# A fused decoder step on one core: value products of the attention one step later in TensorE's order, and a head's gate behind the decode maximum on VectorE

## The reference

```
def _attend_block(q_lat, q_pe, c_kv, k_pe, q_pos, k_pos):
    s = (einsum('bqhc,bkc->bhqk', q_lat, c_kv)
         + einsum('bqhr,bkr->bhqk', q_pe, k_pe)) * ATTN_SCALE
    s = where(k_pos <= q_pos, s, -inf)
    p = softmax(s, axis=-1)
    return einsum('bhqk,bkc->bqhc', p, c_kv)
...
    o = einsum('bthc,chv->bthv', o_lat, w_uv)
    return (o * silu(gate)) @ w_out
```

## Time and profile before

| | |
|---|---|
| median of 3 runs | 1121.33 us |
| lowest, highest | 1116.54, 1121.57 us |
| profiled execution, its own time | 1121.29 us |
| its span, first to last instruction | 1119.1 us |
| mean granted TensorE clock | 0.967 |
| TensorE busy | 1041.1 us (93%) |
| VectorE busy | 514.5 us (46%) |
| ScalarE busy | 308.0 us (28%) |
| GpSimd busy | 93.8 us (8%) |

### The profile page before, as it was taken

How to read it: one execution, slowest core, us unless ns; L and a number is a source line. 1 busy time by engine, 2 the same in 40 slices (tenths; PEclk the granted TensorE clock), 3 DMA queues, 4 the chain that set the end, 5 groups by cost and what they waited for, 6 DMA issues and landing times.

```text
span 1119.1 us, 26006 instructions
## 1 busy us (share of the span) xinstructions
PE 1041.1 (93%) x11635; PEld 740.6 (66%) x11635; DVE 514.5 (46%) x963; ACT 308.0 (28%) x589; POOL 93.8 (8%) x140
## 2 busy tenths in 40 slices
PE   2697999999999999999999798999899999999996
PEld 0476877767677777767655344888584767666566
DVE  0595445464555546455555786220202354444105
ACT  2213132232322132232210214232223344444102
POOL 0002011010100111010010130000001000100111
PEclk8899999999999999999989898999999899999989
DMA  8601012040402203040050657311324222432102
GB/s 355 232 1 61 17 63 95 2 155 3 150 8 79 79 11 146 2 155 3 11 226 19 246 212 290 152 56 57 109 74 97 76 95 96 146 139 89 63 1 77
DMA packets 19999, 110.49 MB, mean 99 GB/s; under 512 B 7080, under 2 KB 11952, under 8 KB 13872
## 3 DMA queue, kind: packets, MB, share of 16 engines
q1 hardware_dynamic: 13712, 84.62, 20.4%
q0 software_dynamic: 2304, 20.97, 5.2%
q10 hardware_dynamic: 3872, 3.24, 0.9%
HBM read 102.30 MB, written 5.19 MB: 96 GB/s over the span
## 4 chain that ended last, share of the span: by engine, by line
PE 80%; DVE 7%; ACT 2%; issue 2%; DMA 1%; SPq 0%; ACTq 0%; DVEq 0%
PE pj L959 20%; PE pj L1437 7%; PE bk L1069 7%; PE pj L1348 5%; PE pj L1488 3%; PE pj L1201 3%; PE pj L1366 2%; PE bk L1540 2%; PE bk L1468 2%; PE bk L892 2%; PE bk L1524 2%; PE bk L1525 2%; PE bk L1142 1%; PE pj L1553 1%; PE pj L988 1%
## 5 line engine op out<-in xcount | busy, mean ns | idle before, releaser
L959 PE MATMUL pj<-XM,ring 128*128 128x260 f32 x1024 | 261.7, 397 | 0.9 <-DVE XM L1784 0.9
L959 PEld LDWEIGHTS pj<-XM,ring 128*128 128x128 f32 x1024 | 183.7, 190 | 40.7 <-issue 12.1
L1437 PE MATMUL pj<-XM,ring 128*128 128x260 f32 x352 | 79.3, 388 | 2.9 <-ACT XM L777 2.9
L1437 PEld LDWEIGHTS pj<-XM,ring 128*128 128x128 f32 x352 | 67.6, 193 | 14.3 <-issue 3.8
L1069 PEld LDWEIGHTS bk<-arena,ring 64*64 64x64 f32 x2560 | 44.6, 134 | 31.3 <-issue 31.3
L1069 PE MATMUL bk<-arena,ring 64*64 64x64 f32 x2560 | 55.6, 224 | 0.0
L892 PE MATMUL bk<-ring,cT 128*9 128x512 f32 x256 | 35.4, 651 | 20.6 <-DMA ring<-in_ada 20.6
L1877 DVE TENSOR_TENSOR arena<-arena,bk 128x512 f32<-128x512 f32 x40 | 27.5, 688 | 58.5 <-PE bk L1069 58.5
L1871 DVE TENSOR_TENSOR arena<-bk,arena 128x512 f32<-128x512 f32 x40 | 27.7, 692 | 35.6 <-PE bk L1069 35.4
L1201 PE MATMUL pj<-R,ring 128*128 128x512 f32 x64 | 35.2, 665 | 6.2 <-DVE R L1932 4.2
L1841 DVE TENSOR_TENSOR ring<-bk,arena 128x512 f32<-128x512 f32 x32 | 22.1, 689 | 37.2 <-PE bk L1024 36.6
(11 more groups left out here) (352 smaller groups left out, 1729.3 us busy)
## 6 DMA issues: line engine op xcount, KB each, us to landing
ring<-in_ada SPq DMA_DIRECT2D x16, 2048.0 KB, 8.2
ring<-in_w_in SPq DMA_DIRECT2D x8, 2048.0 KB, 7.4
ring<-in_b_w_in SPq DMA_DIRECT2D x3, 2048.0 KB, 11.6
R<-in_xT SPq DMA_DIRECT2D x2, 2080.0 KB, 14.4
ring<-in_w_out SPq DMA_DIRECT2D x2, 2048.0 KB, 8.3
XM<-in_Sd SPq DMA_DIRECT2D x1, 2048.0 KB, 18.2
out_wkv_s<-XM SPq DMA_DIRECT2D x1, 2048.0 KB, 6.4
ring<-in_uk SPq DMA_DIRECT2D x1, 2048.0 KB, 7.9
```

What stands on the lines that cost most here:

```text
L959: last = mm(pj[:, s, a, 0:HALF], w[:, e, k, :], XM[:, e, k, a * HALF:(a + 1) * HALF], start=(k == 0), stop=(k == KT - 1))
L1437: last = mm(pj[:, t % 2, a, 0:HALF], w[:, k, e * P:(e + 1) * P], H1[:, k, a * HALF:(a + 1) * HALF], start=(k == 0), stop=(k == KT - 1))
```

## The change

In TensorE's list the value products of a step are moved into the next step, between its cache scores and its transposes; those of the last step stand behind the last cache scores. In VectorE's list the gate of a finished head is moved from ahead of `row_max` to behind `decode_max`. Nothing is added or removed; the waits that each piece carries are the same.

```
@@ TensorE, the loop over steps
                 if n >= 1:
                     cache_scores(n - 1)
+                if n >= 1:
+                    row_values(n - 1)
                 if s >= 1 and g == 2:
                     turn_weights(s - 1)
                 turn_rows(n)
                 turn_cache(n)
                 if s >= 1 and g == 3:
                     decode_values(s - 1)
-                row_values(n)
             cache_scores(NSTEP - 1)
+            row_values(NSTEP - 1)
             pe.wait_ge(s_pog, H)
@@ VectorE, the loop over steps
-                if s >= 1 and g == 0:
-                    gate_head(s - 1)
                 if n + 1 < NSTEP:
                     row_max(n + 1)
                 if s >= 1 and g == 0:
                     decode_max(s - 1)
+                    gate_head(s - 1)
                 if n + 1 < NSTEP:
                     row_scale(n + 1)
                 cache_turned(n)
```

## The result

| | before | changed |
|---|---|---|
| median of 20 runs | 1119.40 us | 1114.41 us |
| lowest, highest | 1116.54, 1122.87 us | 1112.72, 1120.14 us |
| profiled execution: span | 1119.1 us | 1115.7 us |
| mean granted TensorE clock | 0.967 | 0.972 |
| one head of the attention (four steps) | 19.97 us | 19.12 us |

The ratio of the run times is 0.9959, with a 95% interval from 0.9947 to 0.9972: 4.6 us faster (the medians differ by 5.0 us).

A forecast was written before the change was run, and what follows sets the result against it. TensorE was taken to set the pace, only its idle time winnable: -9.1 (old waits) + 5.9 (new waits) + 0.8 (last gate) + 1.6 (joins) = -0.8 us, from 1121.29 to 1120.5 us; range 1116.5 to 1124.5 us.

The forecast's parts named there:

- the gate had to move: VectorE at g = 0: left ahead, the gate would delay row maximum and decode exponentials; moved, it waits for nothing, 0.8 us slack.
- none at g = 0: TensorE after g = 0: L1572 would not wait for the cache copy L845, 1.68 against 1.47 us, slack 0.21.
- the uncovered last gate: End of the loop: the last gate no longer runs beside the cache scores, so the projection starts later, plus 0.78 us.
- Rival A: TensorE's waits: the old ones for L839 go and no new one comes, 1114.6 us; chance 0.07.
- B: Value products' entry and exit on TensorE each cost another 0.10 us, so the kernel gets slower, 1125.1 us; chance 0.15.
- joins: Extra cost where TensorE changes between groups of products, three changes a step: plus 0.05 us a step, plus 1.6 us.
- C: Slack of 0.21 us at g = 0 is missing; the large wait moves from L839 to L845, 1124.0 us; chance 0.08.
- waits for L839: TensorE's value products waiting for ScalarE's copy L839 at g = 0 and g = 2: both go, minus 9.1 us.
- new wait for L845: L1572 waits for ScalarE's cache copy after g = 2, 0.64 us seven times; new waits in all plus 5.9 us.
- In step 13, where nothing is late, it is 0.29 us: TensorE, L1556's start to L1540's: 0.29 us taken as the free distance from which the waits were counted.
- I take plus 0.05, because the value products now sit behind the narrow products, where the dearest join was: TensorE's joins in 31 steps: 0.05 us more a step, from a span of 0.06 less to 0.10 more; plus 1.6 us.
- The Trainium skill's rule: Weight loads overlap running products only in other row groups; loads behind narrow products exposed, 107 ns each, sum 1.7 us higher.

## Why the prediction was wrong

What was right: which wait goes, that the gate had to move and then hides, what takes the place of the old wait and where (L1572 for L845 behind g = 2, none at g = 0), the uncovered last gate, and the direction. Rival A (no new wait) falls: the wait is there, and removing it brings 0.71 us a head. That its time, 1114.6 us, is close to the measured 1114.41 is chance; by the time alone one would have taken it for true. B (dearer joins) has the wrong sign. C fails too: L845 ends at 938.03 and L1572 starts at 938.20, a slack of about 0.12 us where I had 0.21.

What was wrong are sizes, and two steps made them. Per head, in the steady part:

| term | forecast | measured |
|---|---|---|
| waits for L839 | -1.24 | -1.45 |
| new wait for L845 | +0.64 | +0.73 |
| joins | +0.20 | -0.10 |
| sum | -0.40 | -0.82 (period: -0.85) |

First, the step "In step 13, where nothing is late, it is 0.29 us". There L839 was 0.07 us late. The free distance is 0.22 us, so each of the three waits before was larger (1.02, 0.07 and 0.36 us), and the new one is 1.49 - 0.22 - 0.54 = 0.73. Net 0.12 us a head.

Second, and larger, the step "I take plus 0.05, because the value products now sit behind the narrow products, where the dearest join was". The dear join was already paid there by the transposes, 0.05 us of it in their own pitch, and the value products had paid the larger restart in their old place, behind a wait in three steps and behind the narrow decode_values in the fourth. Moved, they pay it behind the cache scores, and the transposes no longer do: from L1531 to L1556 are 0.99 us (935.61 to 936.60) where 1.04 were the earlier trace rows, 0.05 us in each of four steps. Only one place is new: at g = 3 the scores now pay it behind decode_values, 932.78 to 933.84 being 1.06 us against 0.96, plus 0.10. Net -0.10 us a head instead of +0.20.

Over the whole attention, counted in the same way, the waits for L839 were about 10.6 us (forecast 9.1), the new ones are about 6.6 (5.9) and the uncovered gate 0.8 (0.8). What is left of the measured 4.39 us is a gain of about 1.2 us by joins, where the forecast had a loss of 1.6. So the joins are 2.8 us of the 3.6 us by which the attention's gain was forecast too small. Heads 2 to 6 gained 0.85 us each (counted between the L1524 of 256 columns) and head 1 0.61 us, since it carries the wait behind head 0's last step, 0.3 us. Head 0's gain of 0.83 us and the last stretch's loss of 1.22 us can't be read by themselves: the last four value products of a head, about 1.0 us, now stand behind the L1524 from which the next stretch is counted, so the first stretch has lost them and the last one has them in addition.

The range was too tight below for a reason of its own too: it was placed on three runs whose median was 1.9 us too high. Moved by that it would have begun at 1114.6 us, still just above what was measured.

The Trainium skill's rule, TensorE: Matmul & The Clock Gate, section "The mechanism", would have made the sum higher. The traces don't bear that out: behind narrow products the value products cost 0.10 us above their plain 0.11 each, the same as behind a wait with no product running. And the profile gives each of their weight loads 0.19 us, while the products follow one another at 0.11 in the same rows of the array. How a load and a running product share the array, no run here separates.

## What to carry to other kernels

Before a distance between two instructions is called free, look whether a releaser ended within 0.1 us of the second one's start; a view that lists waits drops short ones (0.05 to 0.15 us here), and every term that is built on the distance inherits the error. When work is moved from behind a producer to cover one wait, ask what it used to cover there: here it had covered the next copy, and an order that leaves it ahead of the copy's reader at the one step that needs it gained 0.71 us a head more. And try the order of the releasing engine first: one call moved on ScalarE, in the kernel before, took 9.4 us off the attention's stretch, where the change took 4.4.

## What the runs showed of the hardware

The first full-width group behind products with 8 columns of weights, or behind a wait, was longer by 0.10 us for value products (two counted products 0.32 against 0.22 us, eight 0.99 against 0.89) and for scores (256 columns 1.06 against 0.96 us). Transposes with the identity were longer by 0.05 us behind such narrow products (0.16 against 0.11 for one); behind a wait none was seen. In a run of full-width groups a counted 128-column product takes 0.11 us. The last full-width group ahead of narrow products took 0.10 us more too: the second score product of 256 columns 0.53 us where the first took 0.43 (L1524 at 934.03, L1525 at 934.46, L1572 at 934.99 in the kernel before). Which part of the engine causes these was not settled.
